# Loads moved from ScalarE's queue to GpSimd's, one 288-column latent projection, and memory squares summed on VectorE

## The reference

```
x        = x + gate2 * swiglu(h, ...)            # end of layer 0
hk       = modulate(rms_norm(x, kv_norm_g), k_shift, k_scale)
kv_a     = hk @ w_kv_a                           # 1024 -> 256 + 32
c_kv, k_rope = split(kv_a, [256])
c_kv     = rms_norm(c_kv, kv_a_norm_g);  kv = c_kv @ w_kv_b   # keys and values of 16 heads
k_rope   = apply_rope(rms_norm(k_rope, k_rope_norm_g), cos(positions), sin(positions))
h        = modulate(rms_norm(x, norm1_g[1]), shift1, scale1)
q        = rms_norm(h @ w_dq, q_norm_g) @ w_uq
mem_n[l] = rms_norm_2(mem, mem_norm[l])          # l = 0, 1; 256 memory rows of 1024
k, v     = split(mem_n[l] @ w_mem_kv[l])
```

## Time and profile before

| | us |
|---|---|
| median of three runs | 1178.94 |
| profiled execution, first to last instruction (span) | 1177.6 |
| TensorE busy | 1138.2 (97%) |
| VectorE busy | 479.5 (41%) |
| ScalarE busy | 286.7 (24%) |
| GpSimd busy | 53.7 (5%) |
| stage of the change, end of the first SwiGLU to the expansion to heads | 368.1 to 414.6 |

### The profile page before, as it was taken

How to read it: one execution, slowest core, us unless ns; L and a number is a source line. 1 busy time by engine, 2 the same in 40 slices (tenths; PEclk the granted TensorE clock), 3 DMA queues, 4 the chain that set the end, 5 groups by cost and what they waited for, 6 DMA issues and landing times.

```text
span 1177.6 us, 19431 instructions
## 1 busy us (share of the span) xinstructions
PE 1138.2 (97%) x8453; PEld 954.6 (81%) x8453; DVE 479.5 (41%) x972; ACT 286.7 (24%) x684; POOL 53.7 (5%) x70
## 2 busy tenths in 40 slices
PE   7888999999999999999999999999999999999997
PEld 5647888888887857688888888888899888887686
DVE  8985544344225328522000000417563542604531
ACT  6512500000004265512000000243122331203432
POOL 3110011011000000000000000000003000000000
PEclk9899999999999999999999999999999999999999
DMA  9994799998833342354445351543420003543220
GB/s 296 327 348 146 253 349 343 367 350 319 306 108 116 134 151 93 100 187 141 146 135 187 107 179 36 172 130 123 147 86 4 4 2 124 199 143 107 74 71 36
DMA packets 122019, 195.64 MB, mean 166 GB/s; under 512 B 5796, under 2 KB 104782, under 8 KB 115534
## 3 DMA queue, kind: packets, MB, share of 16 engines
q1 hardware_dynamic: 110778, 131.15, 34.7%
q0 software_dynamic: 9360, 59.77, 13.0%
q10 hardware_dynamic: 1796, 3.47, 1.0%
HBM read 191.50 MB, written 1.05 MB: 163 GB/s over the span
## 4 chain that ended last, share of the span: by engine, by line
PE 85%; DVE 11%; ACT 2%; issue 1%; DMA 0%; ACTq 0%; DVEq 0%; SPq 0%
PE psum L655 64%; PE psum L1026 13%; DVE arena L1697 4%; PE psum L930 2%; PE psum L1496 1%; DVE sq L1697 1%; ACT arena L2510 1%; DVE arena L1703 1%; DVE arena L1866 1%; DVE xT L1703 1%; PE psum L1471 1%; DVE arena L1960 1%; PE psum L1261 1%; ACT sq L2510 1%; PE psum L1606 1%
## 5 line engine op out<-in xcount | busy, mean ns | idle before, releaser
L655 PE MATMUL psum<-hT,ring 128*128 128x256 f32 x1392 | 309.8, 380 | 1.0 <-DVE hT L1703 0.8
L655 PEld LDWEIGHTS psum<-hT,ring 128*128 128x128 f32 x1392 | 262.2, 190 | 39.5 <-issue 4.9
L2510 ACT ACTIVATE arena<-psum 128x256 f32<-128x256 f32 (+5 forms) x215 | 96.5, 474 | 642.9 <-PE psum L655 590.1
L655 PE MATMUL psum<-hT,arena 128*128 128x256 f32 (+1 forms) x960 | 164.8, 344 | 4.2 <-DVE hT L1697 4.2
L655 PEld LDWEIGHTS psum<-hT,arena 128*128 128x128 f32 (+1 forms) x960 | 143.5, 185 | 23.3 <-issue 5.2
L1697 DVE TENSOR_TENSOR arena<-arena,psum 128x256 f32<-128x256 f32 (+1 forms) x75 | 39.2, 535 | 264.7 <-ACT arena L2510 235.5
L655 PE MATMUL psum<-arena 64*64 64x64 f32 (+7 forms) x1868 | 105.6, 244 | 0.9 <-ACT arena L2510 0.5
L655 PEld LDWEIGHTS psum<-arena 64*64 64x64 f32 (+3 forms) x1868 | 84.5, 141 | 15.0 <-issue 11.1
L1026 PE MATMUL psum<-arena,ring 128*128 128x256 f32 x384 | 85.1, 380 | 0.0
L1026 PEld LDWEIGHTS psum<-arena,ring 128*128 128x128 f32 x384 | 72.6, 190 | 11.0 <-issue 1.2
L655 PE MATMUL psum<-ring,arena 128*128 128x256 f32 (+2 forms) x288 | 73.2, 415 | 0.5 <-ACT arena L2510 0.5
(11 more groups left out here) (257 smaller groups left out, 1167.8 us busy)
## 6 DMA issues: line engine op xcount, KB each, us to landing
aring<-in_ada_w POOLq DMA_DIRECT2D x36, 1024.0 KB, 8.4
ring<-in_a_w_in SPq DMA_DIRECT2D x14, 1024.0 KB, 5.3
arena<-in_ffn_w_gate SPq DMA_DIRECT2D x12, 1024.0 KB, 7.5
arena<-in_ffn_w_up SPq DMA_DIRECT2D x12, 1024.0 KB, 7.9
ring<-in_ffn_w_down SPq DMA_DIRECT2D x12, 1024.0 KB, 5.0
ring<-in_ffn_w_gate SPq DMA_DIRECT2D x10, 1024.0 KB, 9.3
ring<-in_ffn_w_up SPq DMA_DIRECT2D x10, 1024.0 KB, 7.4
arena<-in_ffn_w_down SPq DMA_DIRECT2D x10, 1024.0 KB, 5.0
```

Of the source, the lines that this page charges most:

```text
L655: return eng.matmul(dst, w, x, start=first, stop=last)
L2510: return eng.activation(dst, x, f, **k)
```

## The change

Three edits, in one diff:

1. All DMAs that ScalarE issued in the middle of the program are issued by GpSimd, each group behind a wait of its own: the SwiGLU's last read (positions and gain rows), the query squares (mask rows), the second SwiGLU's last read (RWKV loads), the residual add (last layer's loads). The constants at the start of the program stay on ScalarE.
2. `w_kv_a` is loaded as 7 chunks of 288 columns and an eighth, instead of 256 columns and 32 columns of all chunks; `kva` is 16 products of 288 columns.
3. ScalarE squares the memory in four instructions; VectorE adds the squares with `sum_squares` into one tile, and TensorE multiplies `ones` with that tile alone, between the two halves of `cqt`. ScalarE's root of it moves behind the first `cqt` square.

```diff
-        weights.append((w_kva[:, :, 0:RKV], (KC, RKV), ("kva", 1)))
-        weights.append((w_kva[:, :, RKV:], (KC, DR), ("kva", 1)))
+        KVA_SPLIT = KC - 1
+        for ks in (slice(0, KVA_SPLIT), slice(KVA_SPLIT, KC)):
+            weights.append((w_kva[:, ks, :], (ks.stop - ks.start, RKV + DR), ("kva", 1)))
...
-            def mean_square(key, chunks, src, sig, count, pool="a"):
...
+            def mean_of_sum(key, pool="a"):
                 eng.wait_ge(*next_bank(key, pool))
                 eng.wait_ge(done("square_sums"), SUMS.index(key) + 1)
                 mm(bank_of(key)[:, 0:T], ones, square_sum).then_inc(*fills(key))
...
-                    mm(ps[:, 0:RKV], hT3[:, k, b * P:(b + 1) * P], w[:, k, :], k == 0, k == KC - 1)
...
-                    last = mm(ps[:, RKV:RKV + DR], hT3[:, k, b * P:(b + 1) * P], w[:, k, :], k == 0, k == KC - 1)
+                    w = kva_w[0][0][:, k, :] if k < KVA_SPLIT else kva_w[1][0][:, k - KVA_SPLIT, :]
+                    last = mm(ps[:, 0:RKV + DR], hT3[:, k, b * P:(b + 1) * P], w, k == 0, k == KC - 1)
             row_columns(7, row_late, "b")
-            mean_square("ms_mem", KC, mem_sq, "mem_squares", lambda k: 1, "b")
             w, landed = panel()
             eng.wait_ge(*landed)
             for b in range(2):
+                if b:
+                    mean_of_sum("ms_mem", "b")
                 eng.wait_ge(*next_bank(("cqt", b)))
...
             ada_bias(7)
+            sum_squares("mem_squares", 0, (1, 2, 3), mem_sq)
             inverse_root("ms_mem")
...
-            eng.dma_start(pos_i.bitcast(I32), a["positions"][0].rearrange("(b p) -> p b", p=P),
...
-            act(flat(mem_sq), flat(memT), ACT.Square).then_inc(*s.signals("mem_squares"))
+            for pair in range(4):
+                two = slice(2 * pair, 2 * pair + 2)
+                act(flat(mem_sq[:, two, :]), flat(memT[:, two, :]), ACT.Square).then_inc(*s.signals("mem_squares"))
...
-                if i == 4:
+                if i == 5:
                     root("ms_mem")
...
+            eng.wait_ge(*emptied_at(("dn", 0, 3)))
+            eng.dma_start(pos_i.bitcast(I32), a["positions"][0].rearrange("(b p) -> p b", p=P),
...
+            eng.wait_ge(done("q1_mean"), 2)
+            for x, at in ((qh, CONST_HIDDEN), (kh, CONST_HIDDEN + T)):
...
+            eng.wait_ge(*emptied_at(("dn", 1, 3)))
+            for r, x in ((0, "a_w2_2"), (64, "a_a2_2")):
...
+            eng.wait_ge(done("post_added"), KC)
+            eng.dma_start(alibi, constants[:, CONST_ALIBI:].rearrange("p (h b t) -> p h b t", b=2, t=T))\
```

More of the change, by code:

```diff
@@ L1152, in _ @@
                 eng.wait_ge(*next_bank(("kva", b)))
-            w, landed = panel()
-            eng.wait_ge(*landed)
+            kva_w = [panel() for _ in range(2)]
+            eng.wait_ge(*kva_w[0][1])
             for b in range(2):
@@ L1159, in _ @@
                         eng.wait_ge(done("h_ready"), KC + k + 1)
-                    mm(ps[:, 0:RKV], hT3[:, k, b * P:(b + 1) * P], w[:, k, :], k == 0, k == KC - 1)
+                        if k == KVA_SPLIT:
+                            eng.wait_ge(*kva_w[1][1])
+                    w = kva_w[0][0][:, k, :] if k < KVA_SPLIT else kva_w[1][0][:, k - KVA_SPLIT, :]
+                    last = mm(ps[:, 0:RKV + DR], hT3[:, k, b * P:(b + 1) * P], w, k == 0, k == KC - 1)
+                last.then_inc(*fills(("kva", b)))
+            row_columns(7, row_late, "b")
             w, landed = panel()
@@ L2885, in _ @@
             squares(3)
-            for r, x in ((0, "a_w2_2"), (64, "a_a2_2")):
-                eng.dma_start(w2a2[r:r + 64, :], a[x][0]).then_inc(done("w2_landed"), 16)
-            eng.dma_start(masks7, constants[:, CONST_MASK:CONST_ALIBI]).then_inc(done("masks7_landed"), 16)
             root(("ms", 4))
@@ L3099, in _ @@
             eng.dma_start(mem_nat, a["mem_2"][0].rearrange("(b p) d -> p b d", p=P)).then_inc(done("mem_landed"), 16)
+            eng.wait_ge(*emptied_at(("dn", 0, 3)))
+            eng.dma_start(pos_i.bitcast(I32), a["positions"][0].rearrange("(b p) -> p b", p=P),
+                          allow_slow_non_contiguous=True)\
+               .then_inc(done("positions_landed"), 16)
+            for m, names in enumerate((("k_nope_norm_g", "k_rope_norm_g"), ("mla_q_nope_norm_g", "mla_q_rope_norm_g"))):
+                for name, lo, hi in zip(names, (0, DN), (DN, DQK)):
+                    x = a[name] if m == 0 else a[name][0]
+                    eng.dma_start(gain_rows[:, m, lo:hi], x.partition_broadcast(P)).then_inc(done("gain_rows_landed"), 16)
+            eng.wait_ge(done("q1_mean"), 2)
+            for x, at in ((qh, CONST_HIDDEN), (kh, CONST_HIDDEN + T)):
+                eng.dma_start(x[DQK:DQK + 2], constants[0:2, at:at + T].unsqueeze(1).to_broadcast([2, H1, T]))\
+                   .then_inc(done("hidden_landed"), 16)
+            eng.wait_ge(*emptied_at(("dn", 1, 3)))
+            for r, x in ((0, "a_w2_2"), (64, "a_a2_2")):
+                eng.dma_start(w2a2[r:r + 64, :], a[x][0]).then_inc(done("w2_landed"), 16)
+            eng.dma_start(masks7, constants[:, CONST_MASK:CONST_ALIBI]).then_inc(done("masks7_landed"), 16)
             for l in range(2, 6):
@@ L3110, in _ @@
                     .then_inc(*g.signals("level_mask_ahead"))
+            eng.wait_ge(done("post_added"), KC)
+            eng.dma_start(alibi, constants[:, CONST_ALIBI:].rearrange("p (h b t) -> p h b t", b=2, t=T))\
+               .then_inc(done("alibi_landed"), 16)
+            eng.dma_start(post_gain, a["post_norm_2"][1].partition_broadcast(P)).then_inc(done("post_gain_landed"), 16)
 def kernel(**inputs):
```

15 lines of the change are left out of this document (1 added, 14 removed).

## The result

The changed kernel takes 1169.24 us in the median of four runs (1168.66 to 1170.82) against 1179.0 before; the ratio is 0.9916, with a 95% interval of 0.9902 to 0.9930. Predicted were 1169.4 and a range of 1167.6 to 1172.2.

The account below looks back on a forecast made before the run. TensorE was taken to bound the kernel (85% of the span). Savings of 1.50 + 3.11 + 0.44 + 3.91 + 0.55 = 9.51 us from 1178.94 gave 1169.4 us, range 1167.6 to 1172.2 for 8 in 10.

Parts of the forecast that it names:

- root: ScalarE's root of the mean squares: starts earlier once five DMAs leave its queue; 1.50 us, bounds 0 and 1.50.
- projection: Latent projection on TensorE: 16 products of 288 columns take 7.77 us instead of 10.88; 3.11 us saved.
- row transposes: Four TensorE transposes after the projection: at full clock without the 32-column products, 0.88 us halves; 0.44 saved.
- squares: Memory squares on TensorE: one product of 0.43 us replaces eight taking 4.34; 3.91 us saved.
- clock behind the root: TensorE's low clock from 372.50 to 376.20, before the projection: gain between 0 and 1.6 us, 0.55 taken.
- rival with the clock at 2.4 GHz: Clock stays full through the root as TensorE's wait ahead of it goes; 10.6 us saved, 1168.3; chance 0.20.
- queue rival: ScalarE's 1.85 us queue wait was not the DMA's, root hardly earlier; 7.5 us saved, 1171.5; chance 0.12.
- The sum on VectorE: VectorE's added memory squares, wanted by TensorE after cqt's first half: ready in time, slack about 0.2 us.
- late-sum rival: VectorE's sum becomes the bound: a 1 us miss gives 1170.4, no memory gain 1173.3; chance 0.08.
- Positions: Position load issued by GpSimd for VectorE's angles: taken to land after 5 us, at cost 0.
- late positions: Rival: GpSimd's position load lands late, TensorE waits at the summed squares; 1182 at 25 us landing; chance 0.03.

Follow-up runs that it names:

- x11: The changed kernel run again with no edit; 1169.5 us, ratio 0.9927 to the kernel before.
- x1: The kernel before with only the twelve loads moved from ScalarE to GpSimd; 1174.9 us, ratio 0.9973.
- x2: The kernel before with only the latent projection at 288 columns; 1174.0 us, ratio 0.9965.
- x3: The kernel before with only the memory's squares added by VectorE first, 32-column products kept; 1176.2 us, ratio 0.9985.
- x4: The changed kernel with the loads left on ScalarE (288-column projection and VectorE's sum kept); 1172.5 us, ratio 0.9947 to the kernel before.
- x7: The changed kernel with three more ScalarE copies of a memory tile ahead of the root, making TensorE wait; 1169.75 us, ratio 0.9935 to the kernel before.
- x5: The changed kernel with GpSimd issuing positions and gains only after ScalarE's last shifted chunk for cqt; 1171.9 us, ratio 0.9947 to the kernel before.
- x6: The kernel before with three products of 256 columns filling TensorE's wait ahead of the spread; 1175.8 us, ratio 0.9981.
- x8: The changed kernel with ScalarE's copy of the last memory tile moved behind the projection's eight shifts; 1169.97 us, ratio 0.9934 to the kernel before.
- x10: The changed kernel with only positions and four gains on GpSimd, the other seven loads back on ScalarE; 1170.3 us, ratio 0.9924 to the kernel before.

## Why the prediction was right

Its terms, against the profiled stage: root 1.50, measured 1.50; projection 3.11, measured 3.04 (10.87 - 7.83; 7.77 was the estimate for 32 records of 288 columns, 7.83 came); row transposes 0.44 and 0.44; squares 3.91 and 3.91; clock behind the root 0.55, measured 1.36 (4.27 - 2.91) in one execution and 0.27 in the other (x11). Sum 9.51, measured 10.25 and 9.12 (47.58 - 38.46). The medians differ by 9.7. In the profiled execution it was thus the rival with the clock at 2.4 GHz that came (10.6 worked out), in x11 nearer the forecast. The root, the projection and the squares came as they were worked out. The clock's term was a guess between two bounds, and that the whole came so near is in part luck, as the next paragraphs show.

*Root.* Shown by x1: nothing but the loads moved, and the root was at once 0.04 us behind its input. The queue rival is refuted. That the stand recurred with sizes of its own where the loads stayed (root at 4.29 to 4.92) says that the saving is 0.9 to 1.5, not a constant.

*Clock behind the root.* The size was left open and was rightly bounded (0 to 1.6). The reason given for the rival, that the stand precedes the fall, is not borne out. With a stand of 0.8 us or more the clock fell in all five kernels that had it (before, x2, x3, x4, x7). But in x4 and x7 the fall began ahead of the stand, and in x2 and x3 the four records right behind the stand still took the 0.71 us that they take in the changed kernel; only in before may the two coincide. Without a stand the clock fell in four (x1, x5, x6, x11) and stayed up in three (changed, x8, x10), one of them the same program as x11. In the four the stage began at 364.8 to 365.7 us, in the three at 367.7 to 368.1. So the gain is a fall that costs less (x4 and x7 against x11), and perhaps a better chance of none; five of five against four of seven does not show that. What decides in a single execution stays open.

*Row transposes and squares.* The prediction laid the fall to the 32-column products. Where they were kept, it came in two of four (before and x3; not in x1 and x6); where they were gone, in none of eight. That fits, but with one execution of each kernel it is not shown, and products of 32 columns alone are not enough: at 57.34 to 61.20 us in before, 128 records of 32 columns run at 1.00, and so does what follows. Those come every 0.03 us, the projection's every 0.11. The price of a fall is in the term: of the 10.25, 1.36 + 0.37 + 0.41 + 0.89 = 3.0 us are a clock that fell in that profile of before; at full clock the three edits are worth the other 7.2. The sum came out also because it was made against an execution with both falls, which is luck; against x1's, with no fall at the transposes, the projection would have been worth 2.67 (10.50 - 7.83) and the squares 3.02 (3.45 - 0.43).

*The sum on VectorE.* The sum was there 0.44 us ahead of TensorE, or 0.30 if the 0.14 us are counted that the prediction gave to TensorE's seeing it; it had worked out 0.2. ScalarE's squares ended when they were expected (382.85 against 382.8): their pieces took 0.54 each, not 0.60, but began at 380.68, not 380.38. What made the difference is that VectorE began to add at 383.03, where 383.3 was taken. The late-sum rival is refuted here, and x5 shows what it would have cost.

*Positions.* 5 us taken, 2.4 to 3.0 measured: less than the 3.4 of the same load on ScalarE's queue. That late positions make TensorE stand is real (x5), but a landing after 22 us is far away. The five issues took 0.54 to 0.72 us each, the first two beside VectorE's additions and a small scaling, the others beside almost nothing; in x5, with VectorE idle for the first four of them, they took the same 0.54 to 0.72, so the additions cost them nothing. The Trainium skill states in "SBUF — State Buffer", "Who interferes with whom", that VectorE in a two-port mode keeps GpSimd from writing the descriptors of its DMAs. That is neither contradicted nor tested here: no long TENSOR_SCALAR ran beside these issues, and the 1.35 us of the earlier trace rows did not recur.

## What to carry to other kernels

In these traces a small DMA issue costs the issuing engine's queue mostly 0.4 to 0.7 us, and on ScalarE one of five in a row over 1 us; ahead of an instruction on the critical path, five of them are worth moving, far from it seven are not. Products of 32 columns cost 3.9 us of their own here, of which merging them into 288 columns left 0.9; behind them the clock fell in two executions of four, and in none of eight without them, which makes them suspect and no more. Price an edit against more than one execution of the kernel before: a clock that happened to be low in the one profile is counted as a gain. Judge steps of a microsecond inside the stage, by differences between two fixed instructions of one trace, since whole times scatter by more than they are worth.

## What the runs showed of the hardware

The granted clock fell while TensorE was busy without a gap (x1, 0.59 over 4.17 us; x6, 0.54 over 3.24 us); what ran before these falls were 20 records of one column. Behind the same records it stayed at 1.00 in three executions, one of them of the same program as x11, where it fell (stage 37.33 and 38.46 us). Behind the stand of 2.80 us in x5, with products of 256 and 288 columns ahead of it, it was down too: 0.67 over `cqt`'s second half (387.43 to 392.57), which took 5.30 us instead of 3.62. In before, x2, x3, x4 and x6 one of five small DMA issues in a row on ScalarE's queue took 1.22 to 1.85 us, the third or the fourth of them, and the others 0.39 to 0.49.
